# Seven block products for one quad of more chunks: five of the down projection and three of output projections

## What is computed

```python
    return (jax.nn.silu(gate) * o) @ w_out                       # layers a and b: h = h + this
...
        mixed = g_nsa * (o_nsa @ w_up_nsa[l]) + g_dn * (o_dn @ w_up_dn[l])
        x = x + mixed @ w_o[l]                                   # layer c
        h2 = rms_norm_2(x, norm2_w[l])
        x = x + (jax.nn.silu(h2 @ w_ffn_gate[l]) * (h2 @ w_ffn_up[l])) @ w_ffn_down[l]   # part d, D_FF = 5632
    return rms_norm_2(x, norm_f_w)
```

## Time and profile before

| | us |
|---|---|
| median of 3 runs | 2229.48 (2229.16 to 2229.59) |
| the profiled execution | 2230.15 |
| its span, first to last instruction | 2228.8 |
| TensorE busy | 2208.3 (99%) |
| VectorE busy | 1529.6 (69%) |
| ScalarE busy | 1216.5 (55%) |

### The profile page before, as it was taken

The page is one execution under the profiler, slowest core; times in us unless marked ns, Lnnn a source line. Parts: engine busy times, 40 slices in busy tenths (PEclk is TensorE's granted clock), DMA queues, the critical chain, the costliest instruction groups (busy, mean ns, idle before and its releaser), DMA issues.

```text
span 2228.8 us, 29092 instructions
## 1 busy us (share of the span) xinstructions
PE 2208.3 (99%) x11376; PEld 1825.2 (82%) x11376; DVE 1529.6 (69%) x2034; ACT 1216.5 (55%) x1682; POOL 115.6 (5%) x101
## 2 busy tenths in 40 slices
PE   9999999999999999999999999999999999999998
PEld 7888888888888887888888888888888888888886
DVE  5687765767765677675755556768887578855885
ACT  5545665645665664464544546556555355543554
POOL 0002210003220121000000000000000000000000
PEclk9999999999999999999999999999999999999999
DMA  7456677655677675444644446776666665665674
GB/s 257 143 176 177 196 195 232 202 189 173 201 212 233 195 209 143 142 133 147 223 161 151 151 151 196 231 213 190 210 234 200 203 197 187 214 229 177 202 243 150
DMA packets 313386, 427.31 MB, mean 192 GB/s; under 512 B 121057, under 2 KB 121217, under 8 KB 313121
## 3 DMA queue, kind: packets, MB, share of 16 engines
q1 hardware_dynamic: 311088, 418.35, 59.3%
q0 software_dynamic: 1584, 6.16, 1.0%
q10 hardware_dynamic: 576, 0.95, 0.1%
HBM read 396.06 MB, written 2.10 MB: 179 GB/s over the span
## 4 chain that ended last, share of the span: by engine, by line
PE 92%; issue 3%; DVE 2%; ACT 1%; DMA 1%; POOL 1%; SPq 0%; DVEq 0%; ACTq 0%; POOLq 0%
PE ACC L1127 19%; PE ACC L1129 19%; PE ACC L1128 19%; PE ACC L988 3%; PE ACC L989 3%; PE ACC L990 3%; PE SCPV L988 3%; PE SCPV L989 3%; PE SCPV L990 3%; PE SCPV L1060 1%; PE ACC L1059 1%; PE SCPV L1058 1%; PE SCPV L1059 1%; PE ACC L1060 1%; PE ACC L1058 1%
## 5 line engine op out<-in xcount | busy, mean ns | idle before, releaser
L2257 DVE TENSOR_TENSOR WL<-W,WH 128x1024 fp32r<-128x1024 f32 x729 | 894.0, 1234 | 399.3 <-ACT WH L1156 165.8
L1156 ACT ACTIVATE WH<-W 128x1024 fp32r<-128x1024 f32 x729 | 744.8, 1049 | 248.7 <-PE ACC L1129 93.6
L1127 PE MATMUL ACC<-WH,XH 128*128 128x512 f32 x1888 | 764.9, 405 | 4.0 <-ACT arena L1156 3.0
L1129 PE MATMUL ACC<-WH,XL 128*128 128x512 f32 x1888 | 737.1, 390 | 0.0
L1128 PE MATMUL ACC<-WL,XH 128*128 128x512 f32 x1888 | 735.4, 389 | 0.0
L1127 PEld LDWEIGHTS ACC<-WH,XH 128*128 128x128 f32 x1888 | 354.8, 188 | 80.9 <-issue 6.0
L1129 PEld LDWEIGHTS ACC<-WH,XL 128*128 128x128 f32 x1888 | 354.3, 188 | 76.5
L1128 PEld LDWEIGHTS ACC<-WL,XH 128*128 128x128 f32 x1888 | 355.2, 188 | 68.9 <-issue 1.2
L1156 ACT ACTIVATE arena<-arena 128x1024 uint16<-128x1024 uint16 (+5 forms) x98 | 87.1, 893 | 68.9 <-DVE arena L1948 26.0
L1156 ACT ACTIVATE arena<-ACC,reciprocal_roots 128x512 f32<-128x512 f32 x86 | 58.6, 687 | 118.5 <-PE ACC L1129 118.0
L988 PE MATMUL ACC<-WH,XH 128*128 128x512 f32 x264 | 103.2, 391 | 0.0
(11 more groups left out here) (378 smaller groups left out, 2657.5 us busy)
## 6 DMA issues: line engine op xcount, KB each, us to landing
W<-in_w_in SPq DMA_DIRECT2D x84, 1024.0 KB, 5.0
W<-in_a_w_in SPq DMA_DIRECT2D x47, 1024.0 KB, 5.4
W<-in_w_ffn_gate SPq DMA_DIRECT2D x44, 1024.0 KB, 5.4
W<-in_w_ffn_up SPq DMA_DIRECT2D x44, 1024.0 KB, 5.2
W<-in_w_ffn_down SPq DMA_DIRECT2D x44, 1024.0 KB, 5.2
W<-in_b_w_in SPq DMA_DIRECT2D x40, 1024.0 KB, 5.2
W<-in_a_w_out SPq DMA_DIRECT2D x16, 1024.0 KB, 5.8
W<-in_b_w_out SPq DMA_DIRECT2D x16, 1024.0 KB, 6.2
```

Source lines behind the costliest of these rows:

```text
L1127: MM(out, hx, WH[:, k, 0:ch.width], start=q == 0 and k == 0, stop=False)
L1129: ins = MM(out, lx, WH[:, k, 0:ch.width], start=False, stop=last and k == QK - 1)
L1156: return nc.scalar.activation(out, in_, func, **how)
L2257: TT(tiles_of(M.WL[K.pair(n)], ch, half), raw, tiles_of(M.WH[n % 3], ch, half).bitcast(F32), ALU.subtract).then_inc(*did("weights_rest", n ...
```

## The change

The seven products are used in eight more places. `o01`, columns 0 to 1023 of the output projections of a, b and c, becomes a chunk of kind `both`, and so do columns 1024 to 2047 of down 0 and down 1 (`d.p0c23`, `d.p1c23`); each chunk of that kind, down 2's included, gets one block. A double chunk of four quads goes through its row quads in the order 0, 2, 1, 3 and has the block in third place, the one of three quads has it in second place. `pair` and `both` on TensorE become one function, `two_chunks` with `seven_products`; the block's products are added into X by eight joins on VectorE (`joins`). The forms are made anew for every set of tokens: a, b, c, gate and up 0, 1 and 2 (since the buffers of the forms were used in between), down 0, 1 and 2, nine times instead of once, always two quads ahead of the first block on these tokens. Down 0's and down 1's second block uses the forms of the first.

```diff
+ORDERS = {"pair": (0, 1, 2, 3), "both": {3: (0, 1, 2), 4: (0, 2, 1, 3)}}
+PLACES = {"pair": 3, "both": {3: 1, 4: 2}}
...
-        for c in range(NC_D):
-            add(f"{l}.o{c}", one(o, c * CH), "dve", fresh="go." + l if c == 0 else None)
+        add(f"{l}.o01", one(o, 0), "both", quads=8, fresh="go." + l)
+        for c in (2, 3):
+            add(f"{l}.o{c}", one(o, c * CH), "dve")
...
         add(f"d.p{p}c01", one("w_ffn_down_2", 0), "both", quads=2 * n, row0=done * CH, xs="H", fresh=f"h{p}.d")
-        for c in (2, 3):
-            add(f"d.p{p}c{c}", one("w_ffn_down_2", c * CH), "dve", quads=n, row0=done * CH, xs="H")
+        if p < len(FF_PARTS) - 1:
+            add(f"d.p{p}c23", one("w_ffn_down_2", 2 * CH), "both", quads=2 * n, row0=done * CH, xs="H")
+        else:
+            for c in (2, 3):
+                add(f"d.p{p}c{c}", one("w_ffn_down_2", c * CH), "dve", quads=n, row0=done * CH, xs="H")
...
-            if n - 3 in K.pair_of:
-                sp.wait_ge(*at("combined", K.pair_of[n - 3], 4))
+            if n - 3 in K.block_at:
+                sp.wait_ge(*at("combined", K.block_at[n - 3], 4))
...
+    def joins(b, steps):
...
+            if i == 0:
+                dve.wait_ge(*at("product_copied", b))
+                ins = TT(x(0, 0), first, x(0, 0), ALU.add)
+            if i == 1:
+                dve.wait_ge(*at("multiplied", g, 0, 1))
+                dve.wait_ge(*at("join_step", b, 0))
+                ins = TT(first, TP[1][:, :], first, ALU.add)
...
+    def block_work(b, q, half, t):
+        ch, where = K.blocks[b].chunk, (q - 2 * place_of(K.blocks[b].chunk), half, t)
+        first = not any(other.tokens == K.blocks[b].tokens for other in K.blocks[:b])
+        j = int(ch.name[4:]) if ch.taker == "pair" else None
+        if first and where == (-2, 0, 0):
+            forms(b)
+        if where == (-1, 0, 0):
+            combine(b, 1)
+            combine(b, 2)
+        if where == (-1, 0, 1):
+            combine(b, 3)
+        if where == (0, 0, 0):
+            combine(b, 4)
+            combination_rest(b, 2)
+        if where == (0, 0, 1):
+            if j is not None:
+                gate_left(j)
+            combination_rest(b, 4)
+            combination_rest(b, 3)
```

More of the change, by code:

```diff
@@ L150, with order_of, place_of, block_plan @@
 Chunk = namedtuple("Chunk", "name first quads parts width row0 k0 xs fresh taker tiles")
+def order_of(ch):
+    return ORDERS["pair"] if ch.taker == "pair" else ORDERS["both"][ch.quads // 2]
+def place_of(ch):
+    return PLACES["pair"] if ch.taker == "pair" else PLACES["both"][ch.quads // 2]
+Block = namedtuple("Block", "quad chunk tokens source slice room")
+def block_plan(chunks):
+    blocks, part = [], 0
+    for ch in chunks:
+        if ch.taker not in ("pair", "both"):
+            continue
+        if ch.taker == "pair":
+            part = sum(int(ch.name[4:]) >= start for start in FF_STARTS) - 1
+            tokens, source, room = f"gate and up {part}", "x.d", "d"
+        elif ch.xs == "H":
+            tokens, source, room = f"down {part}", f"h{part}.d", "d"
+        else:
+            tokens, source, room = ch.name[0], {"a": "go.a", "b": "go.b", "c": "mx.c"}[ch.name[0]], ch.name[0]
+        place = place_of(ch)
+        blocks.append(Block(ch.first + 2 * place, ch, tokens, source, order_of(ch)[place], room))
+    return blocks
 def weight_plan():
@@ L194, in weight_plan @@
         add(f"c.ud{c}", one("w_up_dn_2", c * CH), "dve", quads=2, k0=8, fresh="od.c" if c == 0 else None)
-    for c in range(NC_D):
-        add(f"c.o{c}", one("w_o_2", c * CH), "dve", fresh="mx.c" if c == 0 else None)
+    add("c.o01", one("w_o_2", 0), "both", quads=8, fresh="mx.c")
+    for c in (2, 3):
+        add(f"c.o{c}", one("w_o_2", c * CH), "dve")
     done = 0
@@ L996, in pair, with seven_products @@
+    def seven_products(ch, x, visit, ends):
+        b, hi, lo = K.block_at[ch.first + 2 * place_of(ch)], M.hi[ch.xs], M.lo[ch.xs]
+        block = K.blocks[b]
+        g, u = block.quad, block.quad + 1
+        tokens = lambda a, t, k: a[:, QK * x + k:QK * x + k + HK, t * P:(t + 1) * P]
         A11, A12, A22 = [(tokens(hi, t, k), tokens(lo, t, k)) for t, k in ((0, 0), (0, HK), (1, HK))]
-        S1, S2, S3, S4 = [(M.form_hi[:, i], M.form_lo[:, i]) for i in range(4)]
-        place = lambda n, half: (M.WH[n % 3][:, half * HK:(half + 1) * HK, :], M.WL[K.pair(n)][:, half * HK:(half + 1) * HK, :])
@@ L1000, in product @@
-        def product(out, form, weights, first=False, last=False):
+        form_hi, form_lo = M.FORMS[block.room]
+        S1, S2, S3, S4 = [(form_hi[:, i], form_lo[:, i]) for i in range(4)]
+        weights = lambda n, half: (M.WH[n % 3][:, half * HK:(half + 1) * HK, :], M.WL[K.pair(n)][:, half * HK:(half + 1) * HK, :])
+        def product(out, form, w, first, last):
             nonlocal visit
             for k in range(HK):
-                MM(out, form[0][:, k, :], weights[0][:, k, :], start=first and k == 0, stop=False)
-                MM(out, form[0][:, k, :], weights[1][:, k, :], start=False, stop=False)
-                ins = MM(out, form[1][:, k, :], weights[0][:, k, :], start=False, stop=last and k == HK - 1)
+                MM(out, form[0][:, k, :], w[0][:, k, :], start=first and k == 0, stop=False)
+                MM(out, form[0][:, k, :], w[1][:, k, :], start=False, stop=False)
+                ins = MM(out, form[1][:, k, :], w[0][:, k, :], start=False, stop=last and k == HK - 1)
@@ L1010, in pair @@
             for half in range(2):
[L1011 removed]
+                pe.wait_ge(*at("turned", ch.fresh, 2 * x + half))
         pe.wait_ge(*at("weights_rest", g, 0))
[L1013 to L1015 removed]
+        wait_empty("PV0")
+        product(PV[0][:, :], A11, weights(g, 0), True, True).then_inc(*did("product", b, 1))
```

393 lines of the change are left out of this document (216 added, 177 removed).

## The result

The changed kernel takes **2255.9 us** (median of 4 runs, 2255.3 to 2257.4), beside 2229.5 us of the kernel before on the same chip: a ratio of 1.0119, 95% interval 1.0102 to 1.0137. The direction was forecast, the size was not: 2246.1 us were predicted, with a range of 2235 to 2254.

A forecast was written before the change was run, and what follows sets the result against it. TensorE was taken to bound the kernel, busy 99%. From 2229.48 us, 11.6 saved against 1.7 (gate and up), 5.7 (projections), 8.2 (down 0, 1) and 12.6 (down 2) gave +16.6: 2246.1 us, range 2235 to 2254.

The forecast's parts named there:

- The sum keeps the clock at 1.00: TensorE's granted clock behind the new waits: assumed not to fall, so no cost for slower matmuls was counted.
- The fall at the end of the kernel: After the last matmul: the granted clock fell to 0.50 some 4 us after TensorE stopped.
- the waits of 4.1 to 4.4 us: Three long waits, in down 0, down 1 and down 2: each only about as long as the clock's fall took.
- the rival: Clock falls in some long waits: 2 us for one, 6 for three, 2248 to 2252, up to 2256 us; 18 in 100.
- The rule of the Trainium skill: Idle TensorE returns to half clock until busy for a while, so waits cost more than their length; no size given.
- The waits: TensorE waits for VectorE, mainly before new blocks' third products; several in down 2, also gate and up 4, 8: 28.2 us.
- a: Projection block of layer a: third product late by 1.8 us behind the forms, 1.9 with the restart.
- down 2: Down 2's block: products late by 3.2, 0.8, 4.4 and 2.1 us, the next quad by 2.1; sum 12.6 us.
- What the matmuls give: TensorE, eight new blocks: 48 matmuls fewer at 0.2267 us, 10.9 us, plus ten chunk-start waits, 0.7; together 11.6 us.
- Moved loads and joins: Later loads and eight joins of 0.69 us: cost nothing, or for the joins about 1 us per block.
- The blocks that find their forms made: Down 0 and down 1, columns three and four: blocks without new forms cost 0.
- The cause of the waits: VectorE ahead of the blocks: forms made nine times instead of once, eight new sets of 4.7 us.

The follow-up runs named there:

- experiment 4: Kernel before, with the third combination computed again 2 to 6 times in seven gate and up blocks to make waits of several lengths: 2269.4 us.
- experiment 5: Kernel before, with the third combination computed again 2 or 3 times in ten gate and up blocks, making waits of 1.55 and 2.81 us: 2261.9 us.
- experiment 1: Changed kernel without the block in down 2, whose sixteen half-quad products return: 2242.4 us, ratio 1.0065 to the kernel before.
- experiment 6: Changed kernel with only the three output projections' blocks, forms in one piece, and down chunks plain: 2234.3 us, ratio 1.0027 to the kernel before.
- experiment 3: Changed kernel with forms spread over visits, down 0 and 1 included, and no block in columns 0 and 1 of the down chunks: 2220.8 us, ratio 0.9965.
- experiment 2: Changed kernel with the forms of projections and gate and up spread one step a visit, down's forms unchanged: 2244.0 us, ratio 1.0068 to the kernel before.
- experiment 7: Changed kernel with forms of every block spread over visits and only down 2 without a block: 2229.2 us, ratio 1.0001 to the kernel before.
- experiment 8: As experiment 7, with projection and down blocks' second and third combinations behind the rests of the block's second quad: 2232.5 us, ratio 1.0015.
- experiment 9: As experiment 1, with projection and down blocks' second and third combinations behind the rests, forms in one piece: 2242.7 us, ratio 1.0060.
- experiment 10: As experiment 8, with down 2's block back and its forms in one piece: 2246.0 us, ratio 1.0072.

## Why the prediction was wrong

**The step that failed** is "The sum keeps the clock at 1.00, because each of them is only about as long as that fall took." The clock fell at five of the waits, and the matmuls behind them were 9.4 us slow. The reason given was wrong twice. The fall at the end of the kernel shows one case, and I took its 4 us for the least that it takes; in down 0 of the changed kernel the level fell after 2.5 us, experiments 4 and 5 show falls at waits of 2.81 us, and experiments 1 and 6 at 1.83 and 1.78. And I counted only the waits of 4.1 to 4.4 us for the rival, so that its price came out as 2 us for each of three (6 us at most) and its chance as 18 in 100. The size of one was right, 1.7 to 2.4 us; it was the number of them that was not. The measured 2255.9 us lie where that rival ended, at 2256, and outside the stated range, which ended at 2254. The rule of the Trainium skill named there (TensorE: Matmul & The Clock Gate, Part 1), that an idle TensorE goes back to half the clock and that waits so cost more than their length, was the case, by these 9.4 us.

**The waits** were right in place and releaser, but for the second product of down 2, which did not wait, and nearly right in sum: 26.8 us where I had 28.2. Mis-sized were a (1.9, measured 3.6; 2.0 where the transfer came in time) and down 2 (12.6, measured 9.5). There the same missed clock is in play: the first two products, at the lower level, took until 2187.9 and not 2186.1 (from 2183.36 it is 2.72 us at full clock; the third started at 2191.13 after a wait of 3.28 us), and so covered 1.8 us of the 5.2 that I had for the second and the third; the sixth was covered in the same way. The slower matmuls of down 2 are 3.5 us, and 3.1 us of waits went for them.

So the profiled times differ by 26.0 us where the sum had 16.6, and the 9.4 us between them are these: the slower matmuls 9.4, a's late transfer 1.7, less the 3.1 us of down 2's waits, and the 1.4 us of the slightly spread matmuls and the rest. That the first term and the whole are equal is chance. The falls are the largest term, 6.3 us net of down 2's waits: an estimate without them is 2255.9 - 6.3 = 2249.6 us, inside the stated range. Without a's late transfer alone it is 2254.2 us, still outside.

**What the matmuls give**, 0.2267 us each and 11.6 us in sum, held: experiment 3 gave 7.8 of 8.2 us. **Moved loads and joins** cost nothing that the traces show: no wait of TensorE in a block is released by a DMA, an X or an SG. **The blocks that find their forms made**, the second of down 0 and of down 1, cost nothing either, as forecast: each took 9.52 us from its first matmul to the one behind it.

**The cause of the waits** I had as the forms. This holds for a, b, c and the gate and up blocks (experiment 2), and for down 0 and down 1 only in part: there forms and combinations together exceed what VectorE had to spare (experiments 7 and 8). Down 2 was only tried with and without its block: as the change has it, it costs some 10 us, and the cause of each of its waits is argued from the order and the timeline, not tested. Not tried was a second pair of buffers for part d's forms, which could then be made ahead of the last gate and up block's end.

## What to carry to other kernels

Work that is taken from the engine that bounds a kernel is worth its issue time there; work that is put on a helper is free only up to the idle time that this helper has in the stretch ahead of the point where it is waited for. Read that from the windows of the stretch (21.0 of 26 us busy, against 8.2 us of new work), not from the page's mean (69%). Where the helper has room but the work comes in one piece, spread it (11.4 us here, by the ratios of the changed kernel and of experiment 2, up to 3.4 us of it a's late transfer and the fall with it); where it has none, leave the change out in that place (8.0 us), since another order only moved the wait here. And a wait of TensorE of 3 us is to be priced at its length and some 2 us for the clock, one of 2 us at its length and a share of that.

## What the runs showed of the hardware

The fall of the clock by the length of TensorE's wait, over all waits of 1.5 us and more between the first projection and the end of the work, all traces together: behind 1.55 us none of 6; behind 1.78 to 2.12 us 3 of 10 (b in one run, a in another, with the same code); behind 2.3 to 2.95 us in experiments 8 to 10 4 of 8; behind 2.81 us in experiments 4 and 5 6 of 7; behind 3.0 us and more 18 of 18. In 24 of the 31 falls the matmuls behind it are 1.4 to 1.9 us slow, most often 1.7, and in 7 they are 2.3 to 3.0 us slow, because the low stretch was longer (the waits at 1639.68 and 1916.02 in experiment 4 are two of them). In all these 7 the level had fallen 0.7 us or more before TensorE began again; in the other 24 it fell at most 0.6 us before that, or up to 1.2 us after it, with the wait already over. So a wait that makes a product 1.9 to 2.0 us late costs 2.1 us (b) or 3.7 us (a in experiment 1), with the matmuls behind it; what decides it for a given one these runs leave open.

The idle time in a row's brackets is less than what the wait costs. It is counted from the recorded end of the matmul before, 0.39 us after its start, where the next would have started after 0.2267 us. So the third product of b is 1.94 us late for 1.78 us idle, and the matmuls behind it lose 0.13 us more.

A slow stretch is not always added in full: where a second wait follows it closely, as in down 2, the slow matmuls fill a part of that wait.
